# Earlier places for the copies out of the gather buffers in the decode loop of a hybrid decoder layer

## The reference

```python
def nsa_cmp_slc(q, rows, qpos, cmp_w1, cmp_w2, cmp_pe, blocked):
    kc = compress(rows[:, :, 0], cmp_w1[0], cmp_w2[0], cmp_pe[0])
    vc = compress(rows[:, :, 1], cmp_w1[1], cmp_w2[1], cmp_pe[1])
    o_cmp, p = cmp_attention(q, kc, vc, qpos)
    kb = to_blocks(rows[:, :, 2])
    vb = to_blocks(rows[:, :, 3])
    sel = select_blocks(p, qpos, kb.shape[2])
...
        o_slc = selected_attention(q, kb, vb, sel, qpos)
    return o_cmp, o_slc
```

## Time and profile before

| | us |
|---|---|
| median of 3 runs | 2246.21 (2242.72 to 2254.63) |
| the profiled execution, its own time | 2249.45 |
| its span in the trace | 2247.6 |
| PE busy in the span | 2016.1 (90%) |
| DVE, ACT, POOL busy | 915.7, 707.9, 629.6 |
| mean granted clock of TensorE, share of full speed | 0.955 |

### The profile page before, as it was taken

One profiled execution on the slowest core, in us unless ns is written; L12 is line 12 of the kernel. 1 busy time (PEld: TensorE's weight loads), 2 busy tenths in 40 slices (PEclk: granted clock), 3 DMA queues, 4 the chain that ended last, 5 costly groups with the idle time before them and its releaser, 6 DMA issues. The chain is left out here.

```text
span 2247.6 us, 24649 instructions
## 1 busy us (share of the span) xinstructions
PE 2016.1 (90%) x9303; PEld 1372.5 (61%) x9303; DVE 915.7 (41%) x1821; ACT 707.9 (31%) x1297; POOL 629.6 (28%) x649
## 2 busy tenths in 40 slices
PE   8999999999999999999968778677687878899997
PEld 7888888888888877777634334333343434434442
DVE  0445355454510144444434344445353545432126
ACT  0233112332200032332335444445354544510013
POOL 0000000000020034343545465555565555240000
PEclk9999999999999999999979889898888998999999
DMA  5232222222232211111155253545454453564114
GB/s 202 67 101 77 85 85 77 94 75 85 77 111 76 93 61 57 38 57 38 54 177 146 76 159 90 179 121 165 134 144 142 139 155 119 164 234 155 75 75 151
DMA packets 71076, 247.86 MB, mean 110 GB/s; under 512 B 11220, under 2 KB 28832, under 8 KB 56768
## 3 DMA queue, kind: packets, MB, share of 16 engines
q1 hardware_dynamic: 38344, 139.10, 17.8%
q0 software_dynamic: 31360, 103.32, 15.7%
q10 hardware_dynamic: 1280, 4.23, 0.5%
HBM read 224.64 MB, written 21.96 MB: 110 GB/s over the span
## 5 line engine op out<-in xcount | busy, mean ns | idle before, releaser
L292 PE MATMUL pj<-xT,strips 128*128 128x260 f32 x2368 | 532.6, 384 | 6.4 <-DMA xT<-d_xT 6.4
L292 PEld LDWEIGHTS pj<-xT,strips 128*128 128x128 f32 x2368 | 445.9, 191 | 72.3 <-issue 6.3
L1835 ACT ACTIVATE big<-dtb 64x512 f32<-64x512 f32 x512 | 302.8, 591 | 314.6 <-PE dtb L1569 172.2
L792 PE MATMUL pj<-xT,strips 128*128 128x260 f32 x1216 | 292.0, 388 | 0.0
L1592 PE MATMUL dpH<-big,w 128*128 128x512 f32 x512 | 287.3, 658 | 0.4 <-DVE hs L1958 0.4
L792 PEld LDWEIGHTS pj<-xT,strips 128*128 128x128 f32 x1216 | 222.4, 190 | 59.8 <-issue 30.1
L1018 POOL MEMSET kbd<- 128x128 f32 x1 | 0.2, 205 | 635.4 <-POOLq L126 635.4
L1569 PEld LDWEIGHTS dtb<-const,xT 128*128 128x128 f32 x512 | 65.3, 150 | 181.5 <-issue 87.5
L1941 DVE TENSOR_TENSOR big<-big 128x512 f32<-128x512 f32 x128 | 88.3, 689 | 212.5 <-ACT big L1835 174.2
L1569 PE MATMUL dtb<-const,xT 128*128 128x128 f32 x512 | 84.7, 292 | 99.9 <-DVE KgT L1807 79.2
L1044 POOL TENSOR_SCALAR old<-old,rd 128x128 f32<-128x128 f32 (+3 forms) x116 | 122.2, 1068 | 166.6 <-DVE rd L1153 166.6
(11 more groups left out here) (311 smaller groups left out, 2402.1 us busy)
## 6 DMA issues: line engine op xcount, KB each, us to landing
strips<-d_w_in SPq DMA_DIRECT2D x60, 1024.0 KB, 5.3
xT<-d_w_out SPq DMA_DIRECT2D x16, 1024.0 KB, 7.5
d_win_sample<-Wt SPq DMA_DIRECT2D x8, 1024.0 KB
Xr<-d_w_out SPq DMA_DIRECT2D x8, 1024.0 KB, 10.1
Wt<-d_win SPq DMA_DIRECT2D x8, 896.0 KB
xT<-d_xT SPq DMA_DIRECT2D x8, 520.0 KB, 8.9
Sold<-d_state SPq DMA_DIRECT2D x8, 512.0 KB, 5.5
vB<-v_rows ACTq DMA_DIRECT2D x8, 512.0 KB, 7.0
```

The costliest lines, as they stand in the source:

```text
L292: mm = nc.tensor.matmul(pj[b][:, a, 0:TH], w[b][:, k, :], xT[:, k, a * TH:(a + 1) * TH], start=(k == 0), stop=(k == KT - 1))
L792: mm = nc.tensor.matmul(bank(s)[:, n, 0:TH], w[s % 2][:, k, :], xT[:, k, n * TH:(n + 1) * TH], start=(k == 0), stop=(k == KT - 1))
L1835: ins = A(dst[:, :, :, hd], tb[bank][hd * DH:(hd + 1) * DH].rearrange("p (j h n) -> p j h n", j=2, h=2), ACT.Copy)
```

## The change

Eight numbers of `AT`: the four fetches and the four keys steps come earlier. No instruction is added or taken away, `LAST` stays as it is, and so seven of the eight sequences are changed.

```diff
-            ("second", 2): 51, ("second", 3): 53, "fetch0": 55, "mix": 56, "acc": 57, "keys0": 59,
-            "fetch1": 62, "keys1": 64, "fetch2": 70, "keys2": 71, "fetch3": 80, "keys3": 81,
+            ("second", 2): 51, ("second", 3): 53, "fetch0": 54, "keys0": 55, "mix": 56, "acc": 57,
+            "fetch1": 59, "keys1": 62, "fetch2": 66, "keys2": 70, "fetch3": 72, "keys3": 76,
```

## The result

| | before | after |
|---|---|---|
| median of 4 runs, us | 2247.27 (2242.72 to 2254.63) | 2274.68 (2264.27 to 2277.85) |
| ratio, 95% interval | | 1.0111 (1.0068 to 1.0154) |
| span of the profiled execution | 2247.6 | 2262.4 |

The change makes the kernel 1.1% slower, and the interval lies clear of 1. The profiled execution of after is the fastest of its four, so the 14.8 us between the two spans are the low end of what is to be explained.

A forecast was written before the change was run, and what follows sets the result against it. PE, busy 90% of the span, was taken as the bound, waiting most for DVE's copy of turned keys. Five sequences' -10.5, the sixth's +4.9 and the first's 0 gave -5.6 us on 2249.45, less 3.2 to the median: 2240.6, range 2208 to 2288.

The forecast's parts named there:

- The new run of 16: POOL's gathers of quarters 2 and 3 go without a pause, delaying PE by 5.3 us, between 0 and 9.0.
- the first sequence's run: 21 gathers of quarters 0 to 2 in the first changed sequence, read as costing 9.0 us from fetch 0 to fetch 1.
- The old hold: PE's 10.6 us delay between places 65 and 72; place 72 would come 1.7 us earlier, 6.9 with no new-run cost.
- Keys 0: Fetch 0 at place 54, keys at 55: +1.1 us from a later turn of place 56, -0.5 given back at 59.
- fetch 0 to keys 1: The first two fetches and keys steps, places 54 to 62: terms of +1.1, -0.5 and -0.3 us per sequence.
- Fetch 3 and keys 3: Places 72 and 76: +1.6 us for a copy ahead of turns 73 and 74, -2.6 for work removed later.
- sequence 0: First changed sequence: already has both kinds of gather run, so no change, 0 us (-5 to +5).
- sequence 6: Sixth changed stretch: without the old hold, but gets the new run, +4.9 us.
- Full DMA engines: Rival: PE's delay comes from full DMA engines, so the new run costs nothing; about 2210 us, chance 0.25.
- Joined runs: Rival: row groups 0 and 1 also join into a second run of 16, +6.9 us a sequence; 2294 us, chance 0.20.
- The gathers change nothing: Rival: group 0's release is set by something else, leaving only -0.4 us a sequence; 2243 us, chance 0.15.
- The sixth stretch: Stretch between fetch 0 value copies with no rows left to gather: 94 us, against 104 to 108 in the other five.

The follow-up runs named there:

- g_nowin: Kernel before with the window rows of sequences 1 to 6 copied in only 16 of 512 columns; ratio 1.0019 where the kernel before takes about 2250 us.
- d_gate_again: Changed kernel with quarter 3 of the gathers also waiting for the turn of place 65; 1.0173 against before, on a late (about 2250 us) chip.
- a_f01: Kernel before with only fetch 0, keys 0, fetch 1 and keys 1 at their new places; 1.0061 on a prompt chip, 1.0083 on a late one.
- c_f3: Kernel before with only fetch 3 and keys 3 at their new places; 0.9947 on a prompt chip, 1.0100 on a late one.
- b_f2: Kernel before with only fetch 2 and keys 2 at their new places; 1.0009 on a prompt chip.
- k_shift: Kernel before with POOL's waits ahead of its four row groups each looking at the turn one group later; 1.0176 on a late chip.

## Why the prediction was wrong

The time, 2274.68, is inside the range of 2208 to 2288, but the forecast was 2240.6 with the gain and the null result ahead of a loss, and the loss is clear. The step that failed first is the price of the new run, and with it what the prediction left out: the other runs that the earlier steps make on POOL. By its own steps, for sequences 1 to 4, whose means of before and after are compared:

- **The new run of 16** exists in all, with the idle time of POOL behind it. Its price was the mis-sized term: I took 5.3 us between 0 and 9.0; 57-67 grew by 9.4 (18.1 to 27.5). The high end, what the first sequence's run had cost, was the value to take. Spreading the 9.0 us evenly over "held" us rested on two estimates (12 and 2 us), and this run of 16 cost as much as that one of 21, which had moreover a pause of 1.03 us behind its 13th gather. Sequence 5 had the same run and no hold (19.3 us; POOL waited 2.64 us there), and why is open.
- **The old hold** was to be shortened by 6.9 us. It went completely: 69-74 from 22.7 to 12.8. The step had tied it to group 0 beside the window, by a fixed distance of 12.55 us; g_nowin shows that the hold doesn't need the window. What went was the run: quarter 3 is no longer joined to group 0; in d_gate_again it is joined again, and 69-74 is back at 21.6. Together with the new run, 57 to 74 is -0.5 a sequence against a forecast of about -1.6.
- **Keys 0** was forecast at +0.6 net; 52-57 grew by 2.5. On the prompt chips it is 0.7 to 1.5 us (a_f01 14.9, beside 14.2 in c_f3 and 13.4 in b_f2, which leave it alone), so this sum stood, and the rest goes with PE's late results. But for fetch 0 to keys 1 as a whole the forecast was +0.3 a sequence, 2 us in all, and a_f01 costs 13 us on a prompt chip: this part was priced too low without any hold.
- **Fetch 3 and keys 3** were forecast at -1.0 together. 74 to 93 came out at +1.1. On the prompt chips 82-89 did fall, by 2.3 to 3.3 us (13.2 in c_f3, against 15.5 in a_f01 and 16.5 in b_f2). On the late one groups 2 and 3 partly joined, and 82-89 rose by 2.6. The step priced PE, ACT and DVE, and not what an earlier turn does to POOL's waits.
- **93 to 52** was not priced; it rose by 1.2.

The differences from the forecast (1.9 us for keys 0; 1.1 for 57 to 74; 2.1 for fetch 3 and keys 3; 1.2 for 93 to 52) sum to the 6.3 us between the forecast and the measured +4.3 for a sequence (the forecast's terms give -2.0; its text rounded to -2.1). Sequence 5 gained 4.7, sequence 0 gained 7.1 where 0 was forecast (its second run shrank from 24 gathers to 16), and sequence 6 lost 9.0 where 4.9 was forecast: its run of 16 held, at full price. 4 x 4.3 - 4.7 - 7.1 + 9.0 is 14.4 of the 14.8 us between the spans.

**The rivals.** Full DMA engines is refuted: the new hold came at a share of 0.37 and 0.26, c_f3 on a prompt chip ran at 0.67 with no hold, and without the window's copy the old hold stayed. The Trainium skill, "DMA: Bandwidth & Descriptors", section "Issuing engines are not separate DMA queues", speaks of transfers that interleave; by it this rival was built, and these rows show a hold with the DMA engines mostly idle. Joined runs named the right price (9.0) and the right side, but its condition, groups 0 and 1 without a pause, was not met (2.46 us between them). A join did come, of groups 2 and 3, which no case had. "The gathers change nothing" fell with POOL's run of 16 and the hold behind it.

What the prediction had not asked is whether the hold was a property of the program at all. The sixth stretch without row gathers was read as "no run, no hold"; it could not show that on another chip the runs hold nothing.

## What to carry to other kernels

When a copy that frees a gather buffer is moved earlier, look at GpSimd's own timeline first: which of its pauses goes away, and how many gathers then stand in a row; that, more than the copy's wait, was what this change turned on where runs of gathers hold PE's results. There a pause of 1.1 us of unused work between runs was worth 1.8% together with the early copies (0.4% on a prompt chip). Before records of semaphores are counted, count whether all are there. And price a loop on more than one chip before a hold of 10 us is taken for a dependency.

## What the hardware showed that I had not expected

- The same program took 2145 us and 2250 us on different chips, 4.9% apart, and the decode loop carries the difference: in c_f3 it accounts for 133 of 137 us, a sequence took 92.8 and 110.2 us. In the timelines a gather takes 0.94 to 0.95 us plus 0.30 on both.
- On the late chips PE's results reached ACT, DVE and POOL late while GpSimd issued gathers (single ones by over 20 us, in k_shift), and the last of them 1.4 to 3.9 us after it stopped (after, before, k_shift). ACT's and DVE's results were not late: one of 340 waits in before and after. On the prompt chips no update of PE was late.
- The hold does not need full DMA engines: the share was 0.26 while ACT waited for PE in after, 0.43 in the middle of k_shift's hold.
- On the late chips the traces lack records too: in before 79 of PE's 454 updates and 170 of DVE's 536 between 1300 and 1950 us, on the prompt chips none.
- What is behind it is open: a path that gathers and PE's results share, or the taking of the records themselves, since every execution here was recorded and records are missing just where results are late. The Trainium skill, "NOTIFIC — the notification-queue block", section "Overflow: three behaviours, one of which stalls the engine", says that the block's internal pipeline always holds producers back rather than losing a record inside the block. The missing records alone do not decide for it, and no run here tells the two apart.
